# Attention of the first block's mixers: turns and scores in one block of products, and the meta keys of two heads turned together

## The chip, the cores and the metric

One core of one Trainium2 chip. The metric is device microseconds of one execution on that core. The kernel before took 1831.22 us, the median of three runs (1830.75 to 1831.36).

## What is computed

The reference runs two layers of a first block and two of a second over 256 tokens of width 1024, in fp32. A layer of the first block is a half feed-forward, a mixer, a half feed-forward. The mixer has a gated linear attention and a softmax attention side by side. The change is in the softmax attention of these two mixers: 8 query heads in 4 pairs, 2 key/value heads, head width 64, no mask, and 16 meta tokens ahead of the 256, so that there are 272 keys.

```python
def attention_branch(q, k, v, gq, gk, cos, sin):
    ...
    qh = apply_axial_rope(rmsnorm(qh, gq), cos, sin) * HEAD_DIM ** -0.5
    kh = apply_axial_rope(rmsnorm(kh, gk), cos, sin)
    ...
    def block(qblk):
        s = jnp.einsum('bkgqd,bksd->bkgqs', qblk, kh)
        p = jax.nn.softmax(s, axis=-1)
        return jnp.einsum('bkgqs,bksd->bkgqd', p.astype(vh.dtype), vh)
```

The queries of the meta tokens matter in layer 0 only. In layer 1 their results are not needed, and `LIVE[1]` is the 256 token columns (`TB`) where `LIVE[0]` is all 272 (`TA`).

## The kernel before

**The stream of weights.** Everything is transposed: features on the partitions, tokens on the free axis. Each weight is split in a high and a low fp32r part, ScalarE making the high (L1191) and VectorE the low (L1748), and each 128x128 piece is used in three products (`product`, L560 to L562). A tile of 24 such products is a unit. Units come in a fixed order through all stages, and a semaphore for each counts how far the split is; it runs up to four units ahead.

**The slots of a mixer.** `mixer(l)` runs 50 slots, `at` or `u` = 0 to 49, one unit each, on TensorE (L916), ScalarE (L1490) and VectorE (L2128) alike. Beside the units run three chains, written as generators: the low-rank gates (slots 3 to 6), the gated linear attention `gla` (7 to 34) and `attention` (8 to 38). After the unit of a slot, `step(chains, u)` moves each chain on to its next `yield` (L437). So the order of work on an engine is an order written out by hand: unit, piece of `gla`, piece of `attention`, next unit. `finish` runs a chain out at its last slot. Each engine takes its instructions strictly in this order. The b products, which need the results of attention, are the units of slots 38 to 41.

**Attention on TensorE** (`attention`, L818) uses PSUM banks 5, 6 and 7 (`b_s`, `b_t`, `b_o`). Slots 8 to 13 normalise the heads. In slot 16 of layer 0 the scores of the meta queries of all heads are made at once (L873), and in slot 17 turned (L842). Then come eight steps. Step `s` takes a pair `p = s // 2` of heads and 128 of the 256 queries:
- scores of both heads (L887), in banks 5 and 6, each 128 queries by 272 keys. The two heads lie in the two halves of the partitions, so that the form of the array is 64 rows by 128 columns (the trace's `64*128`);
- one slot later, the turn (`turn`, L836): three transposes for each head (L842), full 128x128 tiles, into the same banks 5 and 6. The first tile covers the 16 meta keys and 112 keys that are turned again with the next tile; `vb`'s rows past the 16th are zero for it;
- for even steps from 2 on, in the block of the scores, the output of the pair before (`output`, L846): three key tiles by two heads (L857), each head in 64 columns of the array (`128*64`), and in layer 0 the meta queries' six small products (L862).

The last output has a slot of its own. `take(b)` makes TensorE wait for whoever last read a bank. An fp32 product shows as two records in the trace, an fp32r product and a full transpose as one.

**Attention on VectorE** (L2060): `softmax` (L2098) takes, for both heads, the maximum (L2103) and its scaled negative (L2105), waits for ScalarE's exponentials, and then takes the reciprocal of the sums (L2108) and scales the probabilities (L2110), all in the slot of the scores. After an output, `low` makes its low part (`b_lo`, L1754). **On ScalarE** (L1414): the exponentials (L1439) and the high part of an output (`b_hi`, L1449) in the slot of the scores, and the copies of a turn from PSUM (`pt`, L1444) in the slot of the turn. `prob` has one buffer for each head, `pt` holds three key tiles by 256 queries for each.

In layer 0 the steps use slots 18 to 33 and the last output slot 34, in layer 1 slots 16 to 31 and 32. `gla` puts its own pieces in slots 7 to 26: transposes of `kinv` (L739), the sums of states (L752), the gated-attention products (L768, L776), their outputs (L788, L794) and sums of squares (L803, L813).

Of the kernel before, what the change touches and what calls it, by code (L numbers as in the profile page):

```python
# [15 lines left out]
P = 128  # L16
# [186 lines left out]
class Chip:  # L203


    def __init__(self, nc, ctx, args):
# [29 lines left out]
        self.lt = nc.alloc_sbuf_tensor_at("lt", [P, 3, P], F32, offset=place - 4 * (UNIT_W + 3 * P))  # L236
        self.all_lo = sb("w_lo", [P, 4, UNIT_W], F32R, 256, 192)
# [41 lines left out]
        self.prob, self.pt = sb("prob", [P, 2, T]), sb("pt", [P, 2, 3, SEQ])  # L279
# [269 lines left out]
def tensor_program(c, k):  # L549
# [268 lines left out]
    def attention(l):  # L818
# [17 lines left out]
        def turn(step, js, bs):  # L836

            for j, b in zip(js, bs):
                pe.wait_ge(*k.at("att_v", ("prob", l, step, j)))
                take(b)  # L840
                for t in range(3):
                    m = pe.transpose(bank[b][:, t * P:(t + 1) * P], c.prob[:, j, whole_tile(t)], c.ident)  # L842
                m.then_inc(*k.up("att_mm", ("turned", l, step, j)))
                free[b] = [("att_a", ("turned", l, step, j))]

        def output(p):  # L846
# [4 lines left out]
            for par in range(2):  # L851
                pe.wait_ge(*k.at("att_a", ("turned", l, 2 * p + 1, par)))
            take(b_o)
            pair = [(par, bank[b_o][64 * par:64 * par + 64, :], 64 * g + 32 * par + 16 * (p % 2)) for par in range(2)]
            for t in range(3):
                for par, o, _ in pair:
                    m = pe.matmul(o[:, TB], c.vb[:, t, g * 64:g * 64 + 64], c.pt[:, par, t, :], start=t == 0, stop=t == 2,  # L857
                                  skip_group_check=True)
# [9 lines left out]
        if live == TA:  # L868
            take(b_s)
            for g in range(2):  # L870
                for par in range(2):
                    r0, hr = 64 * g + 32 * par, slice(64 * par, 64 * par + 64)
                    m = pe.matmul(bank[b_s][r0:r0 + 32, 0:T], c.qb_meta[hr, 2 * g:2 * g + 2, :].rearrange("p a t -> p (a t)"),  # L873
                                  c.kdup[hr, g, :], start=True, stop=True)
# [3 lines left out]
            turn("meta", (0,), (b_t,))  # L878
            yield
        for step in range(8):  # L880
            p, (c0, n) = step // 2, TILES[1 + step % 2]
            for b in (b_s, b_t):
                take(b)
            for par, b in enumerate((b_s, b_t)):

                hr = slice(64 * par, 64 * par + 64)
                pe.matmul(bank[b][:, 0:T], c.qb[hr, p, c0:c0 + n], c.kdup[hr, p // 2, :], start=True, stop=True).then_inc(  # L887
                    *k.up("att_mm", ("score", l, step, par)))
                free[b] = [("att_a", ("exp", l, step, par))]
            if step and step % 2 == 0:  # L890
                output(p - 1)
            yield
            turn(step, (0, 1), (b_s, b_t))
            yield
        output(3)
        yield

# [274 lines left out]
def scalar_program(c, k):  # L1172
# [241 lines left out]
    def attention(l):  # L1414
# [18 lines left out]
        def exp(step, j, b):  # L1433
            s = c.stat[:, 4 * (2 * (step % 2) + j):4 * (2 * (step % 2) + j) + 4] if step != "meta" else c.stat[:, 0:4]
            act.wait_ge(*k.at("att_v", ("max", l, step, j)))
            if step != "meta":
                if step or live == TA and j == 0:
                    act.wait_ge(*k.at("att_mm", ("turned", l, step - 1 if step else "meta", j)))
# [3 lines left out]
        def turned(step, j, b, dst):  # L1442
            act.wait_ge(*k.at("att_mm", ("turned", l, step, j)))
            act.activation(dst, bank[b][:, 0:3 * P].rearrange("p (t n) -> p t n", t=3), ACT.Copy).then_inc(  # L1444
                *k.up("att_a", ("turned", l, step, j)))
# [5 lines left out]
        if live == TA:  # L1451
            exp("meta", 0, b_s)
            yield
            turned("meta", 0, b_t, c.lt[:, :, :])
            yield
        for step in range(8):
            for par, b in enumerate((b_s, b_t)):
                exp(step, par, b)
# [3 lines left out]
            cs = slice(step % 2 * P, step % 2 * P + P)  # L1462
# [1128 lines left out]
```

## Time and profile before

| | before |
|---|---|
| median of three runs | 1831.22 us (1830.75 to 1831.36) |
| the profiled execution | 1833.29 us |
| its span, first to last instruction | 1831.9 us |
| granted TensorE clock, mean | 0.998 |
| TensorE busy | 1816.5 us (99%), 15035 matmuls |
| VectorE busy | 1360.0 us (74%) |
| ScalarE busy | 1046.6 us (57%) |
| DMA | 364.54 MB, mean 199 GB/s |
| ScalarE copies of a turn, L1444 | 33, median 489 ns |
| exponentials, L1439 | 33, median 488 ns |

The profile is one execution. Busy time of TensorE counts overlapping records once; since matmuls are pipelined, what a block of products costs is read from the starts of the records around it.

### The profile page before, as it was taken

The numbers are of one execution on the slowest core, as the hardware profiler recorded it, in microseconds if no ns is written. First come the engines' busy times: TensorE is split into PE (matmuls) and PEld (weight loads), VectorE is DVE, ScalarE is ACT, GpSimd is POOL, SyncE is SP. The second block draws the span as 40 slices with busy tenths as digits, with TensorE's granted clock in tenths as the row PEclk, the third lists the DMA queues.
The fourth block names the chain that finished last, engine by engine and source line by source line (L and its number), as shares of the span: only waits on it lengthen the run. The fifth ranks groups of instructions, "written<-read, shape, count | busy, mean of one in ns | idle before, by whom it ended". The sixth has DMA issues, their size and how long they took to land.

```text
span 1831.9 us, 36007 instructions
## 1 busy us (share of the span) xinstructions
PE 1816.5 (99%) x15035; PEld 1782.6 (97%) x15035; DVE 1360.0 (74%) x2348; ACT 1046.6 (57%) x1735; POOL 3.1 (0%) x9
## 2 busy tenths in 40 slices
PE   9999999999999999999999999999999999999998
PEld 9999999999999999999899999999999999999998
DVE  7887786687776788778677887787877559778754
ACT  6444675664444544458656554676665457666633
POOL 0000000000000000000000000000000000000000
PEclk9999999999999999999999999999999999999999
DMA  8876342357784677543346786354555554455553
GB/s 290 309 278 231 136 139 95 137 201 263 263 300 165 234 266 284 205 142 135 116 161 241 281 295 249 128 176 150 177 184 184 191 178 165 157 181 186 184 184 116
DMA packets 52386, 364.54 MB, mean 199 GB/s; under 512 B 6684, under 2 KB 7356, under 8 KB 11392
## 3 DMA queue, kind: packets, MB, share of 16 engines
q1 hardware_dynamic: 51792, 361.44, 56.4%
q8 instruction: 120, 1.97, 0.4%
q10 hardware_dynamic: 432, 0.79, 0.1%
q14 instruction: 42, 0.34, 0.1%
HBM read 361.15 MB, written 1.05 MB: 198 GB/s over the span
## 4 chain that ended last, share of the span: by engine, by line
PE 88%; DVE 7%; ACT 3%; DMA 1%; issue 1%; SPq 0%; DVEq 0%; ACTq 0%
PE bank L560 26%; PE bank L562 26%; PE bank L561 26%; DVE w_lo L1748 2%; PE bank L620 1%; PE bank L616 1%; PE bank L617 1%; DMA raw_b<-in_weights 1%; ACT w_hi L1191 1%; PE bank L842 1%; PE bank L857 1%; PE bank L887 0%; DVE s_pool L2258 0%; DMA ada_raw<-in_ada_w 0%; PE bank L794 0%
## 5 line engine op out<-in xcount | busy, mean ns | idle before, releaser
L560 PE MATMUL bank<-xn_hi,w_hi 128*128 128x272 f32 (+2 forms) x2640 | 759.1, 288 | 0.3 <-ACT q_all L1660 0.2
L562 PE MATMUL bank<-xn_lo,w_hi 128*128 128x272 f32 (+2 forms) x2640 | 749.7, 284 | 0.0
L561 PE MATMUL bank<-xn_hi,w_lo 128*128 128x272 f32 (+2 forms) x2640 | 749.6, 284 | 0.0
L560 PEld LDWEIGHTS bank<-xn_hi,w_hi 128*128 128x128 f32 x2640 | 498.9, 189 | 8.2 <-issue 4.8
L561 PEld LDWEIGHTS bank<-xn_hi,w_lo 128*128 128x128 f32 x2640 | 498.8, 189 | 0.7
L562 PEld LDWEIGHTS bank<-xn_lo,w_hi 128*128 128x128 f32 x2640 | 498.8, 189 | 0.0
L1191 ACT ACTIVATE w_hi<-raw_a 128x1024 fp32r<-128x1024 f32 (+2 forms) x278 | 302.3, 1088 | 275.0 <-PE bank L562 243.4
L1191 ACT ACTIVATE w_hi<-raw_b 128x1024 fp32r<-128x1024 f32 (+3 forms) x280 | 305.3, 1090 | 269.6 <-PE bank L562 240.8
L1748 DVE TENSOR_TENSOR w_lo<-raw_b,w_hi 128x1024 fp32r<-128x1024 f32 (+3 forms) x280 | 353.5, 1263 | 136.2 <-ACT w_hi L1191 134.0
L1748 DVE TENSOR_TENSOR w_lo<-raw_a,w_hi 128x1024 fp32r<-128x1024 f32 (+1 forms) x276 | 349.0, 1265 | 123.8 <-ACT w_hi L1191 122.7
L560 PE MATMUL bank<-h_hi,w_hi 128*128 128x272 f32 (+1 forms) x704 | 200.8, 285 | 0.4 <-DVE full L1947 0.3
L561 PE MATMUL bank<-h_hi,w_lo 128*128 128x272 f32 (+1 forms) x704 | 200.6, 285 | 0.0
L562 PE MATMUL bank<-h_lo,w_hi 128*128 128x272 f32 (+1 forms) x704 | 200.5, 285 | 0.0
L561 PE MATMUL bank<-f_hi,w_lo 128*128 128x256 f32 x512 | 142.9, 279 | 0.0
L562 PE MATMUL bank<-f_lo,w_hi 128*128 128x256 f32 x512 | 142.9, 279 | 0.0
L560 PE MATMUL bank<-f_hi,w_hi 128*128 128x256 f32 x512 | 142.9, 279 | 0.0
L560 PEld LDWEIGHTS bank<-h_hi,w_hi 128*128 128x128 f32 x704 | 132.5, 188 | 0.9 <-DVE full L1947 0.8
L561 PEld LDWEIGHTS bank<-h_hi,w_lo 128*128 128x128 f32 x704 | 132.5, 188 | 0.0
L562 PEld LDWEIGHTS bank<-h_lo,w_hi 128*128 128x128 f32 x704 | 132.5, 188 | 0.0
L1894 DVE CUSTOM_DVE_ANT_0 ada_raw<-ada_raw,c_rows,bada 128x1024 f32<-128x1024 f32 x96 | 119.3, 1279 | 4.6 <-DMA ada_raw<-in_ada_w 4.6
L560 PEld LDWEIGHTS bank<-f_hi,w_hi 128*128 128x128 f32 x512 | 96.2, 188 | 0.0
L562 PEld LDWEIGHTS bank<-f_lo,w_hi 128*128 128x128 f32 x512 | 96.2, 188 | 0.0
(357 smaller groups left out, 2628.4 us busy)
## 6 DMA issues: line engine op xcount, KB each, us to landing
raw_b<-in_weights SPq DMA_DIRECT2D x120, 1024.0 KB, 4.8
raw_a<-in_weights SPq DMA_DIRECT2D x119, 1024.0 KB, 4.8
ada_raw<-in_ada_w SPq DMA_DIRECT2D x48, 1024.0 KB, 5.1
raw_a<-in_weights SPq DMA_DIRECT2D x16, 1408.0 KB, 5.8
raw_b<-in_weights SPq DMA_DIRECT2D x16, 1408.0 KB, 6.0
raw_b<-in_weights SPq DMA_DIRECT2D x2, 896.0 KB, 4.4
c_rows<-in_c_rows SPq DMA_DIRECT2D x3, 512.0 KB, 6.0
raw_a<-in_weights SPq DMA_DIRECT2D x2, 768.0 KB, 4.1
```

Of the source, the lines that this page charges most:

```text
L560: pe.matmul(o, wh, xh, start=start, stop=False)
L561: pe.matmul(o, wl, xh, start=False, stop=False)
L562: return pe.matmul(o, wh, xl, start=False, stop=stop)
L616: pe.matmul(o, wh[:, s], stream(xh, kk, cols), start=kk == 0, stop=False)
L617: pe.matmul(o, wl[:, s], stream(xh, kk, cols), start=False, stop=False)
L620: m = pe.matmul(o, wh[:, s], stream(xl, kk, cols), start=False, stop=kk == KD - 1)
L842: m = pe.transpose(bank[b][:, t * P:(t + 1) * P], c.prob[:, j, whole_tile(t)], c.ident)
L857: m = pe.matmul(o[:, TB], c.vb[:, t, g * 64:g * 64 + 64], c.pt[:, par, t, :], start=t == 0, stop=t == 2, skip_group_check=True)
L1191: act.activation(weights_of(c, u)[0], raw_of(c, u), ACT.Copy).then_inc(*k.up("w_hi"))
L1748: dve.tensor_tensor(lo, raw_of(c, u), hi.bitcast(F32), ALU.subtract).then_inc(*k.up("w_lo"))
L1894: dve.tensor_tensor_reduce(out=w, in0=w, in1=c.c_rows[:, :], scale=1.0, scalar=c.bada[:, l, n:n + 1], op0=ALU.mult, op1=ALU.add, accum_out ...
```

## The change

1. **Steps of nine.** The loop runs over nine steps of two slots. The first slot of step `s` holds the turn of step `s - 1` and the scores of step `s`, one after the other; the second slot holds the output of pair `s/2 - 1` for even `s`, or nothing. So the turn stands one slot later than before, two units after its scores, and the output one slot later, in a block of its own. The last turn is in slot 34 (layer 0) or 32 (layer 1), the last output one slot on. The meta turn moves from slot 17 to 18, ahead of the first scores.
2. **The turn** goes into bank 7, which the output uses too, and waits for the output's low part. It has four full transposes (two key tiles for each head) and one for the 16 meta keys of both heads: the keys of the first head are stored with the meta tokens last (`kdup`), so that in `prob` the 32 meta columns of the two heads adjoin. This transpose has 32 columns on its stationary side and lands in bank 5, past the scores.
3. **Copies.** ScalarE copies the four tiles at once (128x512), VectorE the 32 rows of the meta keys (`pt_meta`).
4. **The output** has two key tiles by two heads as before, and then one product over the 32 rows of the meta keys for both heads, with `v_pair` (each head's meta values in its half of the columns). ScalarE fills its first half, VectorE its second with two shuffles in each layer.
5. **VectorE's softmax** is split: maxima (and the copy of the turn before) in the first slot, sums and scaling in the second. The exponentials are in the second slot too.
6. Two of the four products of the meta scores are cut in two; VectorE writes the doubled keys in six pieces instead of four.

```diff
-        def turn(step, js, bs):
-            for j, b in zip(js, bs):
+        def turn(step):
+            for j in range(2):
                 pe.wait_ge(*k.at("att_v", ("prob", l, step, j)))
-                take(b)
-                for t in range(3):
-                    m = pe.transpose(bank[b][:, t * P:(t + 1) * P], c.prob[:, j, whole_tile(t)], c.ident)
-                m.then_inc(*k.up("att_mm", ("turned", l, step, j)))
-                free[b] = [("att_a", ("turned", l, step, j))]
+            take(b_o)
+            take(b_s)
+            for j in range(2):
+                for t in range(2):
+                    first = j * META + t * P
+                    pe.transpose(bank[b_o][:, (2 * j + t) * P:(2 * j + t + 1) * P], c.prob[:, j, first:first + P], c.ident)
+            both = c.prob[:, :, :].rearrange("p j t -> p (j t)")[:, N:N + 2 * META]
+            pe.transpose(bank[b_s][0:2 * META, T:T + P], both, c.ident).then_inc(*k.up("att_mm", ("turned", l, step)))
+            free[b_o], free[b_s] = [("att_a", ("turned", l, step))], [("att_v", ("turned", l, step))]
+        def turn_meta():
+            pe.wait_ge(*k.at("att_v", ("prob", l, "meta", 0)))
+            take(b_o)
+            for t in range(3):
+                m = pe.transpose(bank[b_o][:, t * P:(t + 1) * P], c.prob[:, 0, whole_tile(t)], c.ident)
+            m.then_inc(*k.up("att_mm", ("turned", l, "meta")))
+            free[b_o] = [("att_a", ("turned", l, "meta"))]
         def output(p):
             g = p // 2
             if p == 0:
                 pe.wait_ge(*k.at("tile_a", ("vb", l)))
-            for par in range(2):
-                pe.wait_ge(*k.at("att_a", ("turned", l, 2 * p + 1, par)))
+                pe.wait_ge(*k.at("att_v", ("v_pair", l)))
+            pe.wait_ge(*k.at("att_a", ("turned", l, 2 * p + 1)))
+            pe.wait_ge(*k.at("att_v", ("turned", l, 2 * p + 1)))
             take(b_o)
             pair = [(par, bank[b_o][64 * par:64 * par + 64, :], 64 * g + 32 * par + 16 * (p % 2)) for par in range(2)]
-            for t in range(3):
+            for t in range(2):
                 for par, o, _ in pair:
-                    m = pe.matmul(o[:, TB], c.vb[:, t, g * 64:g * 64 + 64], c.pt[:, par, t, :], start=t == 0, stop=t == 2,
-                                  skip_group_check=True)
+                    pe.matmul(o[:, TB], c.vb[:, t + 1, g * 64:g * 64 + 64], c.pt[:, 2 * par + t, :], start=t == 0, stop=False,
+                              skip_group_check=True)
+            m = pe.matmul(bank[b_o][:, TB], c.v_pair[0:2 * META, g, :], c.pt_meta[0:2 * META, :], start=False, stop=True, skip_group_check=True)
 ...
-                    m = pe.matmul(bank[b_s][r0:r0 + 32, 0:T], c.qb_meta[hr, 2 * g:2 * g + 2, :].rearrange("p a t -> p (a t)"),
-                                  c.kdup[hr, g, :], start=True, stop=True)
+                    for at, cs in ((0, slice(0, T)),) if par else ((0, slice(N, T)), (META, slice(0, N))):
+                        m = pe.matmul(bank[b_s][r0:r0 + 32, at:at + cs.stop - cs.start], c.qb_meta[hr, 2 * g:2 * g + 2, :].rearrange("p a t -> p (a t)"),
+                                      c.kdup[hr, g, cs], start=True, stop=True)
 ...
-            turn("meta", (0,), (b_t,))
-            yield
-        for step in range(8):
-            p, (c0, n) = step // 2, TILES[1 + step % 2]
-            for b in (b_s, b_t):
-                take(b)
-            for par, b in enumerate((b_s, b_t)):
-                hr = slice(64 * par, 64 * par + 64)
-                pe.matmul(bank[b][:, 0:T], c.qb[hr, p, c0:c0 + n], c.kdup[hr, p // 2, :], start=True, stop=True).then_inc(
-                    *k.up("att_mm", ("score", l, step, par)))
-                free[b] = [("att_a", ("exp", l, step, par))]
+            yield
+        for step in range(9):
+            if step:
+                turn(step - 1)
+            elif live == TA:
+                turn_meta()
+            if step < 8:
+                p, (c0, n) = step // 2, TILES[1 + step % 2]
+                for par, b in enumerate((b_s, b_t)):
+                    if step:
+                        pe.wait_ge(*k.at("att_a", ("exp", l, step - 1, par)))
+                    else:
+                        take(b)
+                    hr = slice(64 * par, 64 * par + 64)
+                    pe.matmul(bank[b][:, 0:T], c.qb[hr, p, c0:c0 + n], c.kdup[hr, p // 2, :], start=True, stop=True).then_inc(
+                        *k.up("att_mm", ("score", l, step, par)))
+            yield
             if step and step % 2 == 0:
-                output(p - 1)
-            yield
-            turn(step, (0, 1), (b_s, b_t))
-            yield
-        output(3)
-        yield
+                output(step // 2 - 1)
+            yield
 ...
-        def turned(step, j, b, dst):
-            act.wait_ge(*k.at("att_mm", ("turned", l, step, j)))
-            act.activation(dst, bank[b][:, 0:3 * P].rearrange("p (t n) -> p t n", t=3), ACT.Copy).then_inc(
-                *k.up("att_a", ("turned", l, step, j)))
+        def turned(step):
+            act.wait_ge(*k.at("att_mm", ("turned", l, step)))
+            if step == "meta":
+                act.activation(c.lt[:, :, :], bank[b_o][:, 0:3 * P].rearrange("p (t n) -> p t n", t=3), ACT.Copy).then_inc(*k.up("att_a", ("turned", l, step)))
+                return
+            cs = slice(step % 2 * P, step % 2 * P + P)
+            if step > 1 and step % 2 == 0:
+                act.wait_ge(*k.at("att_mm", ("o", l, step // 2 - 1)))
+            act.activation(c.pt[:, :, cs], bank[b_o][:, :].rearrange("p (t n) -> p t n", t=4), ACT.Copy).then_inc(*k.up("att_a", ("turned", l, step)))
 ...
         if live == TA:
+            yield
             exp("meta", 0, b_s)
             yield
-            turned("meta", 0, b_t, c.lt[:, :, :])
-            yield
-        for step in range(8):
-            for par, b in enumerate((b_s, b_t)):
-                exp(step, par, b)
+        for step in range(9):
+            if step or live == TA:
+                turned(step - 1 if step else "meta")
+            yield
+            if step < 8:
+                for par, b in enumerate((b_s, b_t)):
+                    exp(step, par, b)
             if step and step % 2 == 0:
                 output(step // 2 - 1)
             yield
-            cs = slice(step % 2 * P, step % 2 * P + P)
-            for par, b in enumerate((b_s, b_t)):
-                turned(step, par, b, c.pt[:, par, :, cs])
-            yield
-        output(3)
-        yield
 ...
-                    act.activation(c.vb[:, 1:3, :].rearrange("p t n -> p (t n)"), bank[4][:, P:3 * P], ACT.Copy).then_inc(*k.up("tile_a", ("vb", l)))
+                    act.activation(c.vb[:, 1:3, :].rearrange("p t n -> p (t n)"), bank[4][:, P:3 * P], ACT.Copy).then_inc(*k.up("tile_a"))
+                    act.activation(c.v_pair[0:32, :, 0:64], bank[4][0:32, 0:P].rearrange("p (g n) -> p g n", g=2), ACT.Copy,
+                                   scale=c.is_meta[0:32]).then_inc(*k.up("tile_a", ("vb", l)))
 ...
-            for half in range(2):
-                dve.tensor_tensor(c.kdup[64 * half:64 * half + 64, g, :], c.kb[hr, :], f[hr, :], ALU.add).then_inc(
-                    *k.up("att_v", ("rope", l) if g and half else None))
+            for to, cols in ((0, TB), (N, slice(0, META))):
+                dve.tensor_tensor(c.kdup[0:64, g, to:to + cols.stop - cols.start], c.kb[hr, cols], f[hr, cols], ALU.add).then_inc(*k.up("att_v"))
+            dve.tensor_tensor(c.kdup[64:128, g, :], c.kb[hr, :], f[hr, :], ALU.add).then_inc(*k.up("att_v", ("rope", l) if g else None))
         yield
         yield
-        def softmax(step, js, bs):
-            stats = [c.stat[:, 4 * (2 * (step % 2) + j):4 * (2 * (step % 2) + j) + 4] if step != "meta" else c.stat[:, 0:4] for j in js]
-            for j, b, s in zip(js, bs, stats):
+        def stats(step, j):
+            at = 4 * (2 * (step % 2) + j) if step != "meta" else 0
+            return c.stat[:, at:at + 4]
+        def turned(step):
+            cs = slice(step % 2 * P, step % 2 * P + P)
+            if step > 1 and step % 2 == 0:
+                dve.wait_ge(*k.at("att_mm", ("o", l, step // 2 - 1)))
+            dve.tensor_copy(c.pt_meta[0:2 * META, cs], bank[b_s][0:2 * META, T:T + P]).then_inc(*k.up("att_v", ("turned", l, step)))
+        def maxima(step, js, bs):
+            for j, b in zip(js, bs):
+                s = stats(step, j)
                 dve.wait_ge(*k.at("att_mm", ("score", l, step, j)))
+                if step != "meta" and step and j == 0:
+                    turned(step - 1)
                 dve.reduce_max(s[:, 0:1], bank[b][:, 0:T], AX).then_inc(*k.up("att_v"))
                 dve.wait_ge(*k.newest("att_v"))
                 dve.tensor_scalar(s[:, 1:2], s[:, 0:1], -HD ** -0.5, None, ALU.mult).then_inc(*k.up("att_v", ("max", l, step, j)))
-            for j, s in zip(js, stats):
+        def shares(step, js):
+            for j in js:
+                s = stats(step, j)
                 dve.wait_ge(*k.at("att_a", ("exp", l, step, j)))
                 dve.reciprocal(s[:, 3:4], s[:, 2:3]).then_inc(*k.up("att_v"))
                 dve.wait_ge(*k.newest("att_v"))
                 dve.tensor_scalar(c.prob[:, j, :], c.prob[:, j, :], s[:, 3:4], None, ALU.mult).then_inc(*k.up("att_v", ("prob", l, step, j)))
         if live == TA:
-            softmax("meta", (0,), (b_s,))
-            yield
-            yield
-        for step in range(8):
-            softmax(step, (0, 1), (b_s, b_t))
+            maxima("meta", (0,), (b_s,))
+            yield
+            shares("meta", (0,))
+            yield
+        for step in range(9):
+            if step < 8:
+                maxima(step, (0, 1), (b_s, b_t))
+            else:
+                dve.wait_ge(*k.at("att_mm", ("turned", l, 7)))
+                turned(7)
+            if step == 2:
+                dve.wait_ge(*k.at("tile_a", ("vb", l)))
+                for g in range(2):
+                    dve.stream_shuffle(c.v_pair[0:32, g, 64:128], c.v_pair[0:32, g, 0:64], PAIRS).then_inc(*k.up("att_v", ("v_pair", l) if g else None))
+            yield
+            if step < 8:
+                shares(step, (0, 1))
             if step and step % 2 == 0:
                 p = step // 2 - 1
                 hi, lo = (stream(x, p, packed(live)) for x in streams(c, ("b", l)))
                 low(lo, bank[b_o][:, live], hi, ("b", l, p))
             yield
-            yield
-        hi, lo = (stream(x, 3, packed(live)) for x in streams(c, ("b", l)))
-        low(lo, bank[b_o][:, live], hi, ("b", l, 3))
-        yield
```

## Rows read from the trace of the kernel before

**Rows 1.** The page: span, busy engines, TensorE's granted clock by slices, the chain
```profile
span 1831.9 us, 36007 instructions
PE 1816.5 (99%) x15035; PEld 1782.6 (97%) x15035; DVE 1360.0 (74%) x2348; ACT 1046.6 (57%) x1735; POOL 3.1 (0%) x9
PEclk9999999999999999999999999999999999999999
PE 88%; DVE 7%; ACT 3%; DMA 1%; issue 1%; SPq 0%; DVEq 0%; ACTq 0%
```

**Rows 2.** TensorE's timeline, layer 0: start us, us, engine, line, operation; a turn alone
```profile
340.83 0.29 PE L562 MATMUL bank<-xn_lo,w_hi 128*128 128x272 f32 x1
340.95 0.81 PE L842 MATMUL bank<-cst,prob 128*128 128x128 f32 x6
341.53 0.37 PE L560 MATMUL bank<-xn_hi,w_hi 128*128 128x272 f32 x1
341.74 0.28 PE L561 MATMUL bank<-xn_hi,w_lo 128*128 128x272 f32 x1
```

**Rows 3.** Same view: scores alone (layer 1); an fp32 product of 272 columns, then a turn (layer 0)
```profile
290.60 0.62 PE L813 MATMUL bank<-sq,cst 128*128 128x272 f32 x2
291.05 0.82 PE L842 MATMUL bank<-cst,prob 128*128 128x128 f32 x6
...
918.59 0.28 PE L562 MATMUL bank<-xn_lo,w_hi 128*128 128x256 f32 x1
918.80 0.73 PE L887 MATMUL bank<-kdup,qb 64*128 64x272 f32 x4
919.46 0.39 PE L560 MATMUL bank<-xn_hi,w_hi 128*128 128x256 f32 x1
919.68 0.28 PE L561 MATMUL bank<-xn_hi,w_lo 128*128 128x256 f32 x1
```

**Rows 4.** Same view, layer 1: scores and an output in one block; an output alone
```profile
910.02 0.27 PE L562 MATMUL bank<-xn_lo,w_hi 128*128 128x256 f32 x1
910.22 0.73 PE L887 MATMUL bank<-kdup,qb 64*128 64x272 f32 x4
910.88 1.52 PE L857 MATMUL bank<-pt,vb 128*64 128x256 f32 x12
912.55 0.28 PE L561 MATMUL bank<-xn_hi,w_lo 128*128 128x256 f32 x1
...
925.71 0.28 PE L562 MATMUL bank<-xn_lo,w_hi 128*128 128x256 f32 x1
925.92 1.52 PE L857 MATMUL bank<-pt,vb 128*64 128x256 f32 x12
927.59 0.28 PE L561 MATMUL bank<-xn_hi,w_lo 128*128 128x256 f32 x1
```

**Rows 5.** What weight loads waited for, layer 0, then layer 1: us, times, longest
```profile
PEld bank L842 <- DVE prob L2110: 0.7, 3, 0.3
PEld bank L887 <- ACT pt L1444: 0.6, 1, 0.6
...
PEld bank L842 <- DVE prob L2110: 2.0, 5, 1.2
```

**Rows 6.** TensorE's timeline, layer 0: the low-rank products in two column widths
```profile
216.70 0.29 PE L567 MATMUL bank<-xn_lo,lr_both 128*32 128x272 f32 x1
216.82 0.29 PE L566 MATMUL bank<-xn_hi,lr_both 128*64 128x272 f32 x1
```

**Rows 7.** Same view: layer 0, gated-attention products followed by scores
```profile
307.68 2.00 PE L794 MATMUL bank<-qdec,states 64*128 64x16 f32 x32
309.52 0.68 PE L887 MATMUL bank<-kdup,qb 64*128 64x272 f32 x4
```

**Rows 8.** Timelines of TensorE and VectorE, layer 0: second output's end, and its low part
```profile
319.84 0.48 PE L862 MATMUL bank<-lt,vb 128*64 128x16 f32 x12
...
323.56 0.43 DVE L1754 TENSOR_TENSOR b_lo<-bank,b_hi 128x272 fp32r<-128x272 f32 x1
```

More of the change, by code:

```diff
@@ L236, in __init__ @@
         self.lt = nc.alloc_sbuf_tensor_at("lt", [P, 3, P], F32, offset=place - 4 * (UNIT_W + 3 * P))
+        self.v_pair = nc.alloc_sbuf_tensor_at("v_pair", [P, 2, P], F32, offset=place - 4 * (4 * UNIT_W - D))
         self.all_lo = sb("w_lo", [P, 4, UNIT_W], F32R, 256, 192)
@@ L278, in __init__ @@
         place = reused
-        self.prob, self.pt = sb("prob", [P, 2, T]), sb("pt", [P, 2, 3, SEQ])
+        self.prob, self.pt = sb("prob", [P, 2, T]), sb("pt", [P, 4, SEQ])
+        self.pt_meta = sb("pt_meta", [P, SEQ])
         place = end - 8 * N - 64
@@ L1435, in exp @@
             act.wait_ge(*k.at("att_v", ("max", l, step, j)))
-            if step != "meta":
-                if step or live == TA and j == 0:
-                    act.wait_ge(*k.at("att_mm", ("turned", l, step - 1 if step else "meta", j)))
+            if step != "meta" and (step or live == TA):
+                act.wait_ge(*k.at("att_mm", ("turned", l, step - 1 if step else "meta")))
             act.activation(c.prob[:, j, :], bank[b][:, 0:T], ACT.Exp, bias=s[:, 1:2], scale=HD ** -0.5, accum_out=s[:, 2:3]).then_inc(
                 *k.up("att_a", ("exp", l, step, j)))
-        def turned(step, j, b, dst):
-            act.wait_ge(*k.at("att_mm", ("turned", l, step, j)))
-            act.activation(dst, bank[b][:, 0:3 * P].rearrange("p (t n) -> p t n", t=3), ACT.Copy).then_inc(
-                *k.up("att_a", ("turned", l, step, j)))
+        def turned(step):
[7 more added lines that the diff above has]
+            act.activation(c.pt[:, :, cs], bank[b_o][:, :].rearrange("p (t n) -> p t n", t=4), ACT.Copy).then_inc(*k.up("att_a", ("turned", l, step)))
         def output(p):
```

## Prediction

> **What bounds the kernel now.** I began with the page: TensorE is busy 99% of a span of 1831.9 us at the full granted clock (2.4 GHz), and the chain that ended last lies 88% on it, nearly all in the weights' products [rows 1]. A microsecond of TensorE's queue is therefore a microsecond of the kernel. What VectorE and ScalarE do counts only where TensorE waits for it. Next I read TensorE's timeline through both attention stretches (266 to 355 us, layer 0; 852 to 928 us, layer 1). It is a steady row of weights' products, one started every 0.12 us, 24 to a tile, cut by short blocks of the side chains. I price a block so: start of the last weights' product before it to start of the second one after it, less two steps (0.24 us). The second, because the first one after a block starts in a disturbed place.
>
> - A turn, six transposes in full tiles, alone: 341.74 - 340.83 - 0.24 = 0.67 us, 0.11 a transpose, nothing for coming and going [rows 2].
> - Scores, two products on the two row halves, alone: 919.68 - 918.59 - 0.24 = 0.85 us. A 272-column fp32 product is 0.45 us (from L813 to what follows it), and the two halves run together. So 0.3 to 0.4 us is the switch of the array's tile form: 0.09 more than the usual step on entry (0.21 against 0.12), the rest after it [rows 3].
> - An output in layer 1, alone: 927.59 - 925.71 - 0.24 = 1.64 us. Scores and output in one block: 912.55 - 910.02 - 0.24 = 2.29, which is 0.20 less than 0.85 + 1.64. So a full switch there and back is about 0.3 us, a direct switch from one narrow form to another about 0.1, and each join saves 0.2 [rows 4].
>
> Last I read what held TensorE's weight loads: 0.7 + 2.0 us for the probabilities (eight times, one of them 1.2) and 0.6 us for ScalarE's copy of a turn, 3.3 us in all [rows 5].
>
> **Each part.** *Turns.* Sixteen turns (eight in each of two layers) go from six transposes to five: 16 x 0.11 = -1.8 us, if the fifth, whose stationary side is 32 columns wide, costs what a full one does. The trace has no transpose of that form. Nearest below is the full transpose, 0.11. Above it is a plain fp32 product of 128 columns, 0.45 x 128/272 = 0.21, and beyond that the same with a switch of 0.1 to 0.2, up to 0.41. For the switch, the nearest rows are the low-rank products. They go from a 32-column form to a 64-column form and start 0.12 us apart, the usual step, so a change of column width at column group 0 costs nothing there [rows 6]. I take 0.11 and keep 0.21 and 0.41 for the range.
>
> The Trainium skill (TensorEngine Tiling (Array Packing), Key Properties) says that changing the tiling mode drains TensorE. Rows 6 don't show it for column widths, rows 3 do for row halves. By that rule each turn would pay about 0.1 us more, +1.6 in all.
>
> *Outputs.* The third key tile's pair of products (one for each head) becomes one product over 32 rows for both. A pair that runs side by side takes as long as one product, so nothing is won: 1.64 less 0.3 of switching is 1.34, 0.45 a pair, and 0.45 is also one product [rows 3, 4]. But the new one has another form (32 rows, 128 columns). That is one direct switch more in layer 1, and two in layer 0, where the 16-column meta products [rows 8] follow it in the old form: 4 x 0.1 + 4 x 0.2 = +1.2 us. No row has this form; the bound below is no switch, 0.
>
> *Where blocks meet.* Scores of a step stay in their slot between two weight tiles. The turn moves one slot later, ahead of the next step's scores, and the output moves one slot later into a slot of its own. Turn and scores together cost what they did apart, 0.67 + 0.85, because the turn has no switch to save. Six outputs lose their join with the scores; one (layer 0, first pair) finds the gated-attention products in its new slot: 5 x 0.2 = +1.0. In four slots (two in each layer) the scores now follow L794, which has the same form, and start while it still runs [rows 7]. After the change a turn in full tiles stands between the two: out and in again, 4 x 0.3 = +1.2. The meta turn between L752 and the first scores: +0.2. Meta scores: two of four products are cut in two, four more records of 16 columns; L862's twelve take under 0.5 us [rows 8], so +0.1.
>
> *Stalls.* A turn used to follow its scores by one tile, about 2.9 us; in between lie the maximum, the exponential and the scaling, behind whatever else VectorE had. Now two tiles lie between, and VectorE no longer sits through ScalarE's exponential. I take all 3.3 us away.
>
> *New wait.* The turn now writes the output's bank, and waits for the low part of the output that was issued one tile earlier. On TensorE's queue the scores and every weight tile stand behind it, so all of it is on the path. In layer 0 the second output ended at 320.3 and its low part at 324.0, 3.7 us later [rows 8], against a cover of 2.9: 0.8 at such a place. Ahead of that copy ScalarE waited for, and ran, this step's two exponentials, whose maxima are a slot older after the change. I take 0.8 us once, with 0 and six times 0.8 as the bounds.
>
> *Covered.* ScalarE makes one 512-column copy per turn instead of two of 384. VectorE gains a 32-row copy per step, four shuffles, and four more pieces of the doubled keys. Both queues have idle time, and the weights' split runs four tiles ahead of TensorE; were that cover gone, each 0.4 us of VectorE would show as it is. No DMA is added or moved.
>
> **Sum.** TensorE's work: -1.8 + 1.2 + 1.0 + 1.2 + 0.2 + 0.1 = +1.9. Stalls: -3.3 + 0.8 = -2.5. Net -0.6 us. The profiled execution took 1833.29 us and would become 1832.7. The median of the three runs is 1831.22, 2.07 below it, so the forecast against the median is 1830.6 us. That is no change that can be told: about 0.2%, 3.7 us, is what a measurement of this kernel can tell.
>
> **Rivals.**
> - *The narrow transpose is a plain product* (+0.10 each, 16 times: +1.6): net +1.0, 1832.2. With a switch at each as well (+0.30 each): +4.8, net +4.2, 1835.4. For it: no transpose of that form in the trace, and every f32 product takes two records where a full transpose takes one [rows 2, 3]. Against the switch: rows 6. The Trainium skill (TensorEngine Tiling (Array Packing), Gotcha 2: Feature Incompatibilities) states that column tiling excludes the transpose mode for fp32 input, which is the first of these two times; no run here shows it yet. Chances 0.17 and 0.09.
> - *The wait on the output's bank* (the other side: slower than before). At each of the six turns that follow an output by one tile, ScalarE's copy and VectorE's low part come later than 2.9 us. At 0.8 us each it is 4.8 instead of 0.8: net +3.4, 1834.6. It decides as soon as the pair lags by more than one tile. For it: 3.7 us in rows 8. Against: maxima no longer sit inside that lag. Chance 0.1.
> - *Switches cost nothing inside the longer blocks*, and the new wait is nil: TensorE's work -1.8 + 1.0 = -0.8, net -4.1, 1827.1. For it: rows 6; against: rows 4, where the switch is plainly there. Chance 0.14.
> - *The stalls stay*: they move to another wait of the same chain because VectorE is behind, not because the distance is short. Net +2.7, 1833.9. For: the 1.2 us wait came after VectorE's work on the gated-attention heads. Against: a whole further tile. Chance 0.05.
>
> **Numbers.** The forecast's chance is 0.45, for 1829 to 1832. Range 1827.0 to 1835.4: from the free switches to the narrow transpose with a switch. Below 1827.5 is faster by over 0.2%: 0.14. Above 1834.9 is slower by over 0.2%: the 0.09 of the transpose with a switch, and part of the bank's wait, 0.15 together. The rest, 0.71, is no change.
>
> **What would show it.** In the changed profile, TensorE's waits should hold no probabilities and no pt copy. A turn with scores should read 1.5 us by the same pricing, the output alone 1.75 (layer 1) and about 2.2 (layer 0). The transpose with 32 columns should be one record; two mean the first rival. A weight load that waits for b_lo means the second. I am wrong if the blocks from 266 to 355 and from 852 to 928 us together move by more than 4 us, or if the time moves outside them.

## The result, and the profile after

The changed kernel took 1833.23 us (median of 20 runs, 1831.78 to 1837.28), the kernel before 1830.99 us (20 runs, 1829.38 to 1832.91). The ratio is 1.0013, with a 95% interval of 1.0007 to 1.0019: slower by 2.2 us of median, where I had forecast 0.6 us less. The time lies in the range that I gave and within the 0.2% that I had called no change, but twenty runs of each kernel tell it apart from no change, and I had the wrong sign.

The page of the changed kernel:

```profile
span 1831.0 us, 35960 instructions
PE 1817.1 (99%) x15007; PEld 1779.9 (97%) x15007; DVE 1361.4 (74%) x2376; ACT 1041.3 (57%) x1721; POOL 3.1 (0%) x9
PEclk9999999999999999999999999999999999999999
PE 90%; DVE 6%; ACT 2%; DMA 1%; issue 1%; SPq 0%; DVEq 0%; ACTq 0%
```

Beside [rows 1] this says nothing new, and its span is even 0.9 us shorter while the median is 2.2 us longer. Two profiled executions can't be compared by their spans at this size. What can be compared is the start of the same weights' product in both timelines, counted in order (13884 in each; where four in a row stand as one record, they count once). The distance between the two, changed less before, is -0.13 us ahead of layer 0's attention (product 1650, 224.3 us before), +2.16 behind it (product 2400), +1.53 ahead of layer 1's (6000), +1.42 behind it (6900). So attention cost **2.29 us more in layer 0 and 0.11 less in layer 1, 2.2 in all**, which is the difference of the medians. The rest of the way it drifts, most of all by -2.4 us near 1230 us, in the second block's attention, which the change does not touch. There TensorE stood longer in the profiled execution of before; of that kernel:

```profile
PE bank L1004 <- DVE scores L2289: 2.5, 2, 1.9
```

Below, "the stretches" are products 1650 to 2400 and 6000 to 6900, and block prices are read as in the prediction, with steps of 0.1237 us in layer 0 and 0.1167 in layer 1.

What the weights' loads waited for, over the whole changed kernel (us, times, longest):

```profile
PEld bank L562 <- issue: 7.8, 23, 0.6
PEld bank L910 <- issue: 3.1, 15, 0.2
PEld bank L874 <- issue: 3.1, 8, 0.4
PEld bank L847 <- DVE prob L2146: 2.5, 3, 1.1
...
PEld bank L878 <- issue: 1.3, 4, 0.3
```

Two things stand here. The probabilities still hold the turn, 2.5 us against 2.7 in [rows 5], though in three places instead of eight. And there is a line for L874, the new product over 32 rows: eight times 0.4 us in which its weights could not be loaded, with no engine to blame. L878, the meta queries' products behind it, has four more.

TensorE's timeline, changed kernel: a turn with its scores alone, the last output of layer 0, the last of layer 1.

```profile
328.81 0.29 PE L564 MATMUL bank<-xn_lo,w_hi 128*128 128x272 f32 x1
328.94 0.60 PE L847 MATMUL bank<-cst,prob 128*128 128x128 f32 x4
329.38 0.27 PE L849 MATMUL bank<-cst,prob 128*32 128x128 f32 x1
329.58 0.73 PE L910 MATMUL bank<-kdup,qb 64*128 64x272 f32 x4
330.24 0.40 PE L562 MATMUL bank<-xn_hi,w_hi 128*128 128x272 f32 x1
330.47 0.28 PE L563 MATMUL bank<-xn_hi,w_lo 128*128 128x272 f32 x1
...
356.67 0.29 PE L564 MATMUL bank<-a_lo,w_hi 128*128 128x272 f32 x1
356.89 1.08 PE L872 MATMUL bank<-pt,vb 128*64 128x256 f32 x8
357.90 0.69 PE L874 MATMUL bank<-pt_meta,v_pair 32*128 32x256 f32 x2
358.52 0.53 PE L878 MATMUL bank<-lt,vb 128*64 128x16 f32 x12
359.21 0.29 PE L563 MATMUL bank<-a_hi,w_lo 128*128 128x272 f32 x1
...
929.53 0.28 PE L564 MATMUL bank<-xn_lo,w_hi 128*128 128x256 f32 x1
929.73 1.08 PE L872 MATMUL bank<-pt,vb 128*64 128x256 f32 x8
930.75 0.69 PE L874 MATMUL bank<-pt_meta,v_pair 32*128 32x256 f32 x2
931.60 0.28 PE L563 MATMUL bank<-a_hi,w_lo 128*128 128x256 f32 x1
```

The turn is as I had it. The narrow transpose L849 is one record of 0.27 us and starts 0.44 us after the first of the four full ones (0.11 each), so it costs no switch. Turn and scores cost 330.47 - 328.81 - 0.25 = 1.41 us; apart, in [rows 2, 3], they were 1.52. The Trainium skill (TensorEngine Tiling (Array Packing), Gotcha 2: Feature Incompatibilities) excludes the transpose mode for fp32 under column tiling. This trace doesn't agree: the 32-column transpose is one record, at the price of the full one.

The output is not. In layer 1 it costs 1.84 us against 1.64 before [rows 4], in layer 0 2.29 against 1.96 (its last output read in the same way). From L872 to L874 the start moves 1.01 us for products worth 0.85 (two pairs of 256 columns, 0.427 each, which is 256/272 of the 0.45 to 0.46 us that a lone product of 272 columns reads), and L878 starts 0.62 us after L874, a product worth 0.43. Each change of the array's form between two narrow forms takes 0.15 to 0.2 us, where I had put 0.1.

Then the blocks with a wait. TensorE in slot 22 of layer 0, then ScalarE and VectorE ahead of it:

```profile
293.80 0.29 PE L564 MATMUL bank<-xn_lo,w_hi 128*128 128x272 f32 x1
293.93 0.62 PE L815 MATMUL bank<-sq,cst 128*128 128x272 f32 x2
295.29 0.63 PE L847 MATMUL bank<-cst,prob 128*128 128x128 f32 x4 [0.74 <-DVE prob L2146]
295.75 0.27 PE L849 MATMUL bank<-cst,prob 128*32 128x128 f32 x1
```

```profile
291.68 0.43 ACT L1216 ACTIVATE gate<-gate 128x272 f32<-128x272 f32 x1
292.15 0.44 DVE L2072 TENSOR_TENSOR full<-bank,gate 128x272 f32<-128x272 f32 x1 [2.13 <-ACT gate L1216]
292.69 0.50 DVE L2075 SCALAR_TENSOR_TENSOR full<-full,half,r_act 128x272 f32<-128x272 f32 x1
293.23 0.43 ACT L1430 ACTIVATE a_hi<-full 128x272 fp32r<-128x272 f32 x1 [0.82 <-DVE full L2075]
293.56 0.47 ACT L1457 ACTIVATE prob<-bank,stat 128x272 f32<-128x272 f32 x1
293.76 0.44 DVE L1776 TENSOR_TENSOR a_lo<-full,a_hi 128x272 fp32r<-128x272 f32 x1 [0.57 <-ACT a_hi L1430]
294.35 0.36 DVE L2146 TENSOR_SCALAR prob<-prob,stat 128x272 f32<-128x272 f32 x1
294.82 0.36 DVE L2146 TENSOR_SCALAR prob<-prob,stat 128x272 f32<-128x272 f32 x1
```

The maxima of this step were ready at 288.9, but the exponential starts at 293.56: in slot 21 both engines first do a whole head of the gated attention (gate, product, high part, low part), passing it to and fro, and attention's piece comes last in the slot. The turn stands two tiles behind its scores now, but only one behind the slot in which its exponentials are written. This block and its twin in slot 26 cost 2.79 us; 0.46 for the sum of squares and 1.41 for turn and scores are 1.87, so 0.92 us is lost in each. By the blocks, layer 0's waits grew from about 1.3 to 1.8 us; layer 1's fell from about 2.1 to between 0.3 and 0.4.

### The profile page after: what moved, and what is told of

It is laid out like the page before. It is cut to its first block, busy times and chain, and to the rows that moved or that the text cites. A ratio compares the mean times of both kernels' runs of the same rounds, so it can differ in the third digit from the quotient of the medians.

```text
span 1831.0 us, 35960 instructions
## 1 busy us (share of the span) xinstructions
PE 1817.1 (99%) x15007; PEld 1779.9 (97%) x15007; DVE 1361.4 (74%) x2376; ACT 1041.3 (57%) x1721; POOL 3.1 (0%) x9
## 3 DMA queue, kind: packets, MB, share of 16 engines
q8 instruction: 119, 1.95, 0.4%
## 4 chain that ended last, share of the span: by engine, by line
PE 90%; DVE 6%; ACT 2%; DMA 1%; issue 1%; SPq 0%; DVEq 0%; ACTq 0%
PE bank L562 27%; PE bank L564 27%; PE bank L563 27%; PE bank L622 2%; DVE w_lo L1770 2%; PE bank L619 1%; PE bank L618 1%; DMA raw_b<-in_weights 1%; ACT w_hi L1210 1%; PE bank L910 1%; PE bank L847 0%; PE bank L872 0%; PE bank L796 0%; DVE gates L2378 0%; PE bank L1037 0%
## 5 line engine op out<-in xcount | busy, mean ns | idle before, releaser
L563 PEld LDWEIGHTS bank<-f_hi,w_lo 128*128 128x128 f32 x512 | 96.3, 188 | 0.0
```

Source lines behind the costliest of these rows:

```text
L563: pe.matmul(o, wl, xh, start=False, stop=False)
```

## The experiments

The theory after the result has two parts. **Work**: the product over the 32 meta rows of a pair of heads ("the pair" below, with its transpose) costs a switch of form, two in layer 0, each about 0.2 us. **Wait**: in layer 0 the turn waits because its exponentials are last in their slot. The rivals: the output's bank holds the turn, or the loss lies outside the stretches. All runs were timed in five rounds. Ratios are to the kernel before, intervals about 0.09% to either side, so that parts of a microsecond are read from blocks, and a ratio says at most on which side of before a kernel is. Two figures for "the stretches" are the shifts over layer 0's and over layer 1's. What a run saves "less than the changed kernel" is counted from the first profile's +2.29 and -0.11; from the repeat's it would be 0.1 us less.

**The changed kernel again.**

> The changed kernel again, beside which the others are read. Its two attention stretches took 1.8 us more than those of the kernel before by the prices of blocks (layer 0 +2.2, layer 1 -0.4), so the ratio should be 1.001, between 1.0005 and 1.002. If the added time came from outside these stretches (rival), their prices here would not repeat within 0.3 us.

Measured: 1.0008 (1.0000 to 1.0017), 1833.15 us. The stretches: +2.30 and -0.21 us. The two blocks with a wait read 2.80, layer 0's outputs alone 2.29 and 2.30, layer 1's 1.84. Its blocks repeat within 0.02 us, where its span of 1834.4 us is 3.4 above that of the first profile. The loss is in the stretches.

**Attention first in two slots.**

```diff
+def step_late(chains, place, l):
+    step(chains[:1] + chains[:0:-1] if l == 0 and place in (21, 25) else chains, place)
 ...
-            step(chains, at)
+            step_late(chains, at, l)
```

The second part of this edit is made in the mixers of ScalarE and VectorE, not on TensorE.

> Theory: in layer 0 the turns of slots 22 and 26 wait 0.9 us each for the probabilities because ScalarE and VectorE do their piece of the gated attention first in slots 21 and 25. Here attention comes first in these two slots on both engines: the two blocks fall from 2.79 to 1.9 us each, 1.8 us less than the changed kernel, ratio to before about 1.0002. Rival: the turn waits for the output's bank or for the score chain as a whole, then the blocks stay at 2.8 us. A loss elsewhere would show as a wait of the gated attention's sums in slots 22 and 26.

Measured: 1.0003 (0.9994 to 1.0012), 1831.76 us; the stretches +0.70 and -0.21, 1.7 us less than the changed kernel. TensorE in slot 22:

```profile
294.41 0.62 PE L820 MATMUL bank<-sq,cst 128*128 128x272 f32 x2
294.87 0.60 PE L852 MATMUL bank<-cst,prob 128*128 128x128 f32 x4
295.31 0.27 PE L854 MATMUL bank<-cst,prob 128*32 128x128 f32 x1
295.51 0.73 PE L915 MATMUL bank<-kdup,qb 64*128 64x272 f32 x4
```

The turn starts 0.46 us after the sum of squares, with no wait; both blocks cost 1.86 us. The order inside the slot was the cause, and the bank was not: every output and its low part stayed where they were. One place gives 0.2 us back, the output of slot 27 (2.49 for 2.29): TensorE now comes there sooner, and starts 0.10 us behind the end of VectorE's copy of the meta rows, which stands behind a head of the gated attention in slot 26.

**The 32-row product last.** In layer 0's outputs it goes behind the meta queries' products.

```diff
-            m = pe.matmul(bank[b_o][:, TB], c.v_pair[0:2 * META, g, :], c.pt_meta[0:2 * META, :], start=False, stop=True, skip_group_check=True)
             if live == TA:
 ...
+            m = pe.matmul(bank[b_o][:, TB], c.v_pair[0:2 * META, g, :], c.pt_meta[0:2 * META, :], start=False, stop=True, skip_group_check=True)
```

> Theory: a direct switch between two narrow forms of the array costs 0.2 us, not 0.1, and the 32-row product between two 64-column groups pays two. Here it comes last in layer 0's outputs, one switch fewer: the output alone falls from 2.29 to 2.1 us, four times 0.2, 0.8 us in all. If a switch were 0.1 (my prediction) it would be 0.4 us; if the cost is the product's own and not the switch, nothing moves. The ratio cannot tell these, the blocks can.

In this order the kernel does not compute the reference's result (the last section has my reading of it: layer 0's sums over the keys); the products and their sizes are the same. Measured: 1.0008 (0.9999 to 1.0017); the stretches +1.70 and -0.14; the outputs alone cost 2.14 us, 0.15 less each, the other blocks as in the changed kernel. That lies between the two figures that I wanted to tell apart, nearer to 0.2. The same products in another order cost less, so this part of the cost is the switch's and not the product's own.

**The meta queries' products first**, then the two key tiles, then the 32-row product.

> As the kernel with the 32-row product last, but in layer 0 the meta queries' products come first of all, then the two key tiles, then the 32-row product. Again one switch of form fewer in each of four outputs: 0.15 us each, as the run before measured (2.29 to 2.14 us), if the switch is what is saved; block prices elsewhere as in the changed kernel; ratio 1.0005 to 1.0012.

Measured: 1.0012 (1.0003 to 1.0021), the stretches +1.89 and -0.26, the outputs alone 2.18 and 2.19 us, so 0.11 less each; slot 23 3.96 for 4.06. The last output of layer 0:

```profile
356.27 0.53 PE L873 MATMUL bank<-lt,vb 128*64 128x16 f32 x12
356.64 1.06 PE L877 MATMUL bank<-pt,vb 128*64 128x256 f32 x8
357.63 0.69 PE L879 MATMUL bank<-pt_meta,v_pair 32*128 32x256 f32 x2
```

From L877 to L879 it is 0.99 us, 0.14 over the products' 0.85. One switch fewer is worth 0.11 to 0.15 us here. The ratio, as expected, tells nothing.

**Scores ahead of the turn**, in every block, and nothing else on TensorE. VectorE waits for the turn before it copies the meta rows.

```diff
         for step in range(9):
-            if step:
-                turn(step - 1)
-            elif live == TA:
-                turn_meta()
             if step < 8:
 ...
+            if step:
+                turn(step - 1)
+            elif live == TA:
+                turn_meta()
             yield
```

> Scores ahead of the turn in each block. Theory: after the gated attention's products of the same form (slots 20 and 24, both layers) the scores join without a switch, 0.2 to 0.3 us less each, and the turns of slots 22 and 26 in layer 0 have 0.7 us more for their probabilities, so that their wait falls from 0.9 to 0.2. Together 2.2 to 2.6 us less than the changed kernel, ratio 0.9995 to 1.0002. Blocks that stand alone stay at 1.41. Rival (the order inside a block does not matter): no block moves except by the wait.

Measured: 0.9988 (0.9980 to 0.9997), 1829.07 us, faster than the kernel before; the stretches -0.20 and -1.57 us. The scores in slot 24 of layer 0 and what stands around them:

```profile
307.70 2.00 PE L796 MATMUL bank<-qdec,states 64*128 64x16 f32 x32
309.54 0.68 PE L906 MATMUL bank<-kdup,qb 64*128 64x272 f32 x4
310.15 0.66 PE L847 MATMUL bank<-cst,prob 128*128 128x128 f32 x4
310.64 0.27 PE L849 MATMUL bank<-cst,prob 128*32 128x128 f32 x1
310.67 0.37 PE L562 MATMUL bank<-xn_hi,w_hi 128*128 128x272 f32 x1
```

L906 starts while L796 still runs, as in [rows 7]. These four blocks fell by 0.34 us each (4.82 to 4.48, 4.16 to 3.82), the two with a wait from 2.79 to 1.98. I had expected 2.2 to 2.6 us less for the whole, and it was 3.9. Blocks that stand alone fell too, from 1.41 to 1.36, which I had ruled out; the small waits of layer 1 went (1.64 to 1.36 in one); the blocks of slot 18 and of its like in layer 1 fell by 0.19 each. The output of slot 27 rose here too, from 2.29 to 2.48.

**The pair alone, in the old order of steps**: the kernel before, with four full transposes and the narrow one in each turn, and the new output.

```diff
+            both = c.prob[:, :, :].rearrange("p j t -> p (j t)")[:, N:N + 2 * META]
+            pe.transpose(bank[b_t][0:2 * META, 0:P], both, c.ident).then_inc(*k.up("att_mm", ("turned", l, step)))
 ...
+            m = pe.matmul(bank[b_o][:, TB], c.v_pair[0:2 * META, g, :], c.pt_meta[0:2 * META, :], start=False, stop=True, skip_group_check=True)
```

> The kernel before with the meta keys of two heads turned together and nothing moved. Theory: each turn 0.11 us cheaper (16 times, -1.8), each output dearer by its switches (0.2 in layer 1, 0.35 in layer 0, +2.2), meta scores +0.1: +0.5 us, ratio 1.0003, stalls as before (about 3.3 us of weight loads' waits). If the pair were a gain, as the sum of my prediction had it (-1.8 + 1.2 + 0.1), the stretches would be 0.5 us shorter.

Measured: 1.0001 (0.9992 to 1.0010), 1832.33 us; the stretches +0.49 and +0.88, 0.9 more than expected. Turns alone read 0.55 (0.66 before), outputs alone 2.29 and 1.84. By the stretches the pair is a loss by itself (the clock can't tell this kernel from the one before), and its work was priced right; the excess is mostly in waits for probabilities. The longest, in layer 1, beside the 1.0 us of before:

```profile
907.80 0.97 PE L854 MATMUL bank<-cst,prob 128*128 128x128 f32 x4 [1.04 <-DVE prob L2129]
```

This block costs 2.13 where the turn alone costs 0.56, so 1.57 us of waiting against 1.41 in the kernel before. My reading, not tried by itself, is that only two transposes now run while the second head's probabilities are being made, where there were three. The two traces fit it: the weight loads for the second head's tiles waited 0.33 us here and 0.22 before, while the first exponential starts 0.66 us after the first maximum in both.

**The order of steps alone**: the changed kernel with a full transpose of each head's meta tile (past the scores in banks 5 and 6), three key tiles in the output, and the old keys.

```diff
-            pe.transpose(bank[b_s][0:2 * META, T:T + P], both, c.ident).then_inc(*k.up("att_mm", ("turned", l, step)))
+            for j, b in enumerate((b_s, b_t)):
+                m = pe.transpose(bank[b][:, T:T + P], c.prob[:, j, 0:P], c.ident)
 ...
+            for par, o, _ in pair:
+                m = pe.matmul(o[:, TB], c.vb[:, 0, g * 64:g * 64 + 64], c.pt_meta[:, par, :], start=False, stop=True, skip_group_check=True)
```

> The changed kernel with full transposes of each head's meta keys and the old output, so only the order of steps is left of the change. Theory: turn and scores alone 1.52 us, output alone 1.64 (layer 1) and 1.95 (layer 0): 0.4 to 0.5 us less than the changed kernel, ratio to before about 1.001. The two waits of 0.9 us in layer 0 stay. If the pair is what costs the time (rival), this kernel is at or below the one before.

Measured: 1.0012 (1.0003 to 1.0021), 1834.55 us; the stretches +1.80 and -0.03, 0.4 us less than the changed kernel, as expected. Turn and scores alone cost 1.52, outputs 1.95 and 1.64 to the hundredth. The two waits stay (2.90 and 2.91 us for the blocks). Three blocks of layer 1 read 1.71 to 1.72 where 1.52 was due; I had not foreseen those. So the order of steps, as written, costs 1.8 us without the pair.

**Both orders**: attention first in the two slots, and scores first.

> The changed kernel with both orders edited: scores ahead of the turn, and attention first in slots 21 and 25 of layer 0. With scores first alone the two blocks with a wait read 1.98; with this they should read 1.81 (0.45 for the sum of squares, 1.36 for scores and turn), so 0.35 us less than with scores first alone, ratio 0.9980 to 0.9992. If the wait of the turn has another cause, they stay at 1.98.

Measured: 0.9991 (0.9982 to 0.9999), 1829.00 us; the stretches -0.44 and -1.50. The two blocks read 1.81 and 1.82: no wait is left in them. That is 0.32 us less than with scores first alone, as expected. Part of it returns at the output of slot 27, which waits for VectorE's copy of the meta rows:

```profile
321.91 1.08 PE L877 MATMUL bank<-pt,vb 128*64 128x256 f32 x8 [0.18 <-DVE pt_meta L2133]
```

It reads 2.55 us, where scores first alone had 2.48 and the changed kernel 2.29. So layer 0's stretch is 0.24 us shorter than with scores first alone; layer 1's, which the second order does not touch, reads 0.07 longer.

**Both orders and the 32-row product last.**

> The three edits together (attention first in slots 21 and 25 of layer 0, the 32-row product last, scores ahead of the turn). Theory: -1.8, -0.8 and -1.0 to -1.4 from the changed kernel, 3.6 to 4.0 us less, so 1.5 us less than the kernel before, ratio 0.9988 to 0.9995. If the edits only move waits, the ratio stays above 0.9998.

Here too the kernel does not compute the reference's result, for the same order of products. Measured: 0.9984 (0.9975 to 0.9993), 1828.85 us; the stretches -1.03 and -1.41. That is 4.6 us less than the changed kernel, more than the 3.6 to 4.0 expected, because scores first gives more than I had for it.

**Both orders, meta queries' products first.**

> Both orders, and the meta queries' products first in layer 0's outputs. Sum of the parts measured alone: attention stretches 2.4 us shorter than before the change, ratio 0.9980 to 0.9991. If parts overlap in what they win, nearer to 0.999.

Measured: 0.9989 (0.9981 to 0.9998), 1828.70 us; the stretches -0.85 and -1.41, 2.3 us less than before. The parts measured alone gave 2.4: they nearly add up.

**Both orders, without the pair.**

> Both orders, without the pair: full transposes of each head's meta keys and the old output. Theory: turns 0.11 dearer (16 times), outputs 0.2 and 0.35 cheaper (8 times), meta scores 0.04 cheaper: 0.4 to 0.5 us less than the kernel with both orders alone. If VectorE's two copies of 128 rows hold the next block up, as they did in the kernel without the pair (1.71 where 1.52 was due), that is lost again; with scores first the turn is last in its block and the copies have a tile more, so I expect 1.45 to 1.5 us for scores and turn. Ratio 0.9978 to 0.9992.

Measured: 0.9991 (0.9982 to 1.0000), 1829.91 us; the stretches -0.85 and -1.79. Against both orders with the pair the blocks are 0.4 us cheaper in sum (72.49 against 72.87 us from 225 to 372 and from 840 to 942), and scores with turn cost 1.46 to 1.47. A block of it:

```profile
343.08 0.28 PE L568 MATMUL bank<-xn_lo,w_hi 128*128 128x272 f32 x1
343.30 0.73 PE L910 MATMUL bank<-kdup,qb 64*128 64x272 f32 x4
343.96 0.66 PE L851 MATMUL bank<-cst,prob 128*128 128x128 f32 x4
344.45 0.38 PE L853 MATMUL bank<-cst,prob 128*128 128x128 f32 x2
344.80 0.29 PE L567 MATMUL bank<-xn_hi,w_lo 128*128 128x272 f32 x1
```

By its stretches it is the shortest of all that compute the reference, 2.6 us below the kernel before; by the clock the four with scores first can't be told from each other.

## Why the prediction was wrong

- *TensorE bounds the kernel, and the other engines count where it waits*: right. The shift of its products over the two stretches is the difference of the medians, and blocks on its queue hold 1.8 of the 2.2 us.
- *Turns, 16 x 0.11 less, one record, no switch*: right (0.67 to 0.56, L849). Neither form of the first rival came.
- *Outputs, "4 x 0.1 + 4 x 0.2 = +1.2"*: the mis-sized term. They cost 0.20 and 0.34 more, 4 x 0.20 + 4 x 0.34 = +2.2. The step that failed is "a direct switch from one narrow form to another about 0.1". I had taken 0.3 for the switching of one output and left 0.45 for a pair of 256-column products; the pair is 0.427 (by its columns, which I had rounded away), which makes the switching 0.36. With the scores' 0.40, less the 0.20 that a join saves, the switching of a block with both is 0.56; less the entry of 0.09 and the exit of 0.27 (0.36 - 0.09) it leaves 0.2 for the direct switch between them. The rows for it were all in [rows 3, 4].
- *Where blocks meet*: right. Scores behind a turn instead of behind L794 cost 4.82 - 3.98 - 0.55 = 0.29 us against 0.3 taken (3.98 is the like block before, 0.55 five transposes), and undoing it gave 0.34 back with 0.05 from elsewhere. The changed kernel's meta scores read 0.83 against 0.80 before.
- *Stalls, "I take all 3.3 us away"*: the step that turned the sign. They fell from 3.4 to about 2.2 us by blocks. Right for layer 1, wrong for layer 0: I counted tiles between scores and turn, and did not ask in which slot the exponential is written and what stands ahead of it there. The scores' maxima moved a slot ahead of the exponentials, but the turn follows these by one slot as before.
- *New wait, 0.8 us for the output's bank*: did not come at all. Nothing on TensorE waited for b_lo.

Together: work +2.9 instead of +1.9, stalls -1.2 instead of -2.5, so +1.7 by these terms, +1.8 by the blocks' own sum and +2.2 by the stretches, instead of -0.6. The last 0.4 us lies in small irregularities around the blocks that I did not resolve.

Of the rivals, "the stalls stay" was nearest, with a chance of 0.05. It had the right mechanism, another engine behind rather than the distance, in the wrong layer. The range held because it was wide beside the errors (+1.0 us of work, +1.3 us of stalls), which went the same way; that is not support for the sum.

## What to carry to other kernels

Where several chains share hand-written slots, an edit that moves a consumer one slot later buys nothing if its producer moves too: count from the slot in which the last producer is written, and look at what stands ahead of it on its own engine. On a queue that never idles, order products inside a block by the array's form: here putting the scores next to products of their own form, and ahead of the turn that needed time, was worth 3.9 us, while the regrouping that saved one transpose in six cost 0.4 us more, in switches, than it saved. And with executions that scatter by 3 us, align the timelines on the same product and price stretches: here the two spans alone pointed the wrong way.

## What the runs showed that I had not expected

- A direct switch between narrow forms costs 0.11 to 0.2 us: 1.01 us from L872 to L874 for 0.85 us of products; 0.11 and 0.15 us for one switch fewer; 0.20 us for the one in layer 1. The Trainium skill (TensorEngine Tiling (Array Packing), Key Properties) says that changing the mode drains the engine. The trace shows a cost that fits this where rows are split or two column groups are used (0.40 us there and back for scores, 0.36 for an output), and none for a narrow form at column group 0: L849 starts 0.11 us behind the full transposes, and the two forms of [rows 6] start 0.12 us apart.
- The order of scores and turn inside a block that stands alone is worth 0.05 us (1.41 against 1.36), the same in every such block of layer 0.
- The meta queries' products share the output's bank, and the first of them has the start flag. With them between the key tiles and the 32-row product the kernel no longer computed the reference's result; with them ahead of the key tiles it did. That fits the Trainium skill (PSUM — Partial Sum Buffer, The four PSUM rules), by which a starting product clears the marks of what was written over its whole zone of the bank, so that a later product without the flag overwrites; no run here tried it by itself.
